# A two-stream transformer stack on one core: shift products with the shift as the stationary operand, and a re-ordered matrix-memory layer

## The reference, cut to what matters

```
def rms_norm_2(x):
    x32 = x.astype(jnp.float32)
    y = x32 * lax.rsqrt(jnp.mean(x32 * x32, axis=-1, keepdims=True) + EPS)
def modulate(h, shift, scale):
    return h * (1.0 + scale[:, None, :]) + shift[:, None, :]
...
for layer in range(DEPTH_2):
    mod = cond @ ada_w[layer] + ada_b[layer]
    sh1, sc1, g1, sh2, sc2, g2 = jnp.split(mod, 6, axis=-1)
    h = modulate(rms_norm_2(x), sh1, sc1)
    y = mixer(h)                       # pool and attention (layer 0), matrix memory (layer 1)
    x = x + g1[:, None, :] * y
    h = modulate(rms_norm_2(x), sh2, sc2)
    x = x + g2[:, None, :] * swiglu(h, ...)
```

## Time and profile before

| what | value |
|---|---|
| median of 3 runs | 1999.43 us (1997.7 to 1999.89) |
| the profiled execution, its own time | 1998.28 us |
| its span, from first to last instruction | 1996.5 us |
| PE busy | 1927.8 us, 97% |
| DVE, ACT, POOL busy | 938.3, 742.5, 771.6 us |
| mean granted TensorE clock | 0.985 of full speed |

### The profile page before, as it was taken

The page is one execution under the profiler, slowest core; times in us unless marked ns, Lnnn a source line. Parts: engine busy times, 40 slices in busy tenths (PEclk is TensorE's granted clock), DMA queues, the critical chain, the costliest instruction groups (busy, mean ns, idle before and its releaser), DMA issues.

```text
span 1996.5 us, 24687 instructions
## 1 busy us (share of the span) xinstructions
PE 1927.8 (97%) x9394; PEld 1572.7 (79%) x9394; DVE 938.3 (47%) x1227; ACT 742.5 (37%) x921; POOL 771.6 (39%) x225
## 2 busy tenths in 40 slices
PE   6999999989999999979989999999999999999999
PEld 5878778778888888845878888888988787888887
DVE  6244533676614544766776326637844272111111
ACT  5344424443322335236432222244357442222221
POOL 2322314434344444200334443444385344444433
PEclk9999999999999999989989999999999999999999
DMA  4211111436435524100445355422221222223222
GB/s 175 82 64 64 64 64 63 179 100 227 148 117 189 206 100 154 69 4 31 160 168 174 103 176 192 163 97 77 103 86 46 103 84 87 90 87 126 85 79 100
DMA packets 46365, 223.90 MB, mean 112 GB/s; under 512 B 4928, under 2 KB 9280, under 8 KB 31696
## 3 DMA queue, kind: packets, MB, share of 16 engines
q1 hardware_dynamic: 45856, 221.00, 32.4%
q10 hardware_dynamic: 432, 1.84, 0.3%
HBM read 220.68 MB, written 2.13 MB: 112 GB/s over the span
## 4 chain that ended last, share of the span: by engine, by line
PE 52%; issue 34%; POOL 7%; DVE 4%; ACT 2%; DMA 0%; POOLq 0%; DVEq 0%; SPq 0%; ACTq 0%
PE pairs L497 27%; PE pairs L521 10%; POOL wl L2118 7%; PE pairs L540 2%; PE pairs L512 2%; PE pairs L1913 2%; PE pairs L816 2%; DVE arena L438 2%; PE pairs L823 1%; PE pairs L479 1%; PE aux L1900 1%; ACT wh L458 0%; PE aux L881 0%; PE aux L869 0%; DVE xl L448 0%
## 5 line engine op out<-in xcount | busy, mean ns | idle before, releaser
L2118 POOL TENSOR_TENSOR wl<-raw,wh 128x2048 fp32r<-128x2048 f32 (+2 forms) x171 | 706.5, 4132 | 1187.9 <-ACT wh L458 1187.9
L497 PE MATMUL pairs<-xh,wh 128*128 128x512 f32 x1176 | 461.5, 392 | 8.7 <-POOL wl L2118 4.6
L497 PE MATMUL pairs<-xh,wl 128*128 128x512 f32 x1176 | 459.0, 390 | 0.0
L497 PE MATMUL pairs<-xl,wh 128*128 128x512 f32 x1176 | 458.8, 390 | 0.0
L458 ACT ACTIVATE wh<-raw 128x2048 fp32r<-128x2048 f32 x171 | 326.8, 1911 | 341.2 <-PE pairs L521 211.0
L497 PEld LDWEIGHTS pairs<-xh,wh 128*128 128x128 f32 x1176 | 221.7, 189 | 57.8 <-issue 5.3
L497 PEld LDWEIGHTS pairs<-xh,wl 128*128 128x128 f32 x1176 | 221.7, 189 | 46.8 <-issue 1.0
L497 PEld LDWEIGHTS pairs<-xl,wh 128*128 128x128 f32 x1176 | 221.6, 188 | 46.3
L521 PE MATMUL pairs<-zl,wh 128*128 128x512 f32 x518 | 201.6, 389 | 0.0
L521 PE MATMUL pairs<-zh,wl 128*128 128x512 f32 x518 | 201.5, 389 | 0.0
L521 PE MATMUL pairs<-zh,wh 128*128 128x512 f32 x518 | 201.5, 389 | 0.0
(11 more groups left out here) (316 smaller groups left out, 3015.3 us busy)
## 6 DMA issues: line engine op xcount, KB each, us to landing
raw<-in_w SPq DMA_DIRECT2D x113, 1024.0 KB, 5.0
arena<-in_ada SPq DMA_DIRECT2D x96, 512.0 KB, 4.4
raw<-in_w SPq DMA_DIRECT2D x48, 704.0 KB, 4.0
raw<-in_w SPq DMA_DIRECT2D x14, 512.0 KB, 3.7
arena<-mx_rows SPq DMA_DIRECT2D x16, 256.0 KB, 3.5
h<-in_xT SPq DMA_DIRECT2D x4, 512.0 KB, 8.6
outT<-h SPq DMA_DIRECT2D x8, 256.0 KB, 5.4
arena<-in_pool ACTq DMA_DIRECT2D x1, 1024.0 KB, 7.7
```

The costliest lines, as they stand in the source:

```text
L497: mm = p.matmul(pairs[:, 2 * slot + m, :], w[:, slot, at:at + P], src[part][:, k, :], start=(k == 0 and w is wh and part == 0), stop=(k == ...
L2118: g.tensor_tensor(wl[:, slot, 0:w], raw[:, slot, 0:w], wh[:, slot, 0:w].bitcast(F), ALU.subtract).then_inc(lo_done, 1)
```

## The change

It has five parts.

1. Shift products: the two shift columns are loaded as the stationary operand and the weights move, 256 columns at a time. This makes 8 x (wh, wl) = 16 products of 128x256 with a result on 2 partitions (high and low part in a row each). ACT copies that row pair from PSUM to the new tile `shr`, and two products with ones (K=2) turn it into one column per output tile, high and low added; DVE copies the two columns to `wsh`.
2. The place: the 16 products stand right behind `norm_sum_pe` (after k=2) and no longer after k=5; the two new small products stand after k=5. ACT's copy stands ahead of its loop over the tiles (L325).
3. Matrix-memory layer, first unit: its scores are made in the middle of the last `ml_v` chunk, POOL builds its exponents ahead of the low part of `ml_o` chunk 0, and DVE weights its scores ahead of draining that last chunk.
4. Bank pairs swapped: even units use the pair 1, odd units the pair 0. `values(0)` and `values(1)` wait for one chunk of `ml_v` each, and `ml_o` chunk 0 waits for the head sums of unit 14 only; those of unit 15 are waited for ahead of chunk 1.
5. The head copies (every fourth unit) stand behind the head sums and denominators of their round. (Three semaphores of `n_final` become one, with the same order of work.)

```diff
             c0 = C0[NORM_TO[name]]
+            if name in SHIFTED:
+                a.wait_ge(sh_mm, 2 * SHIFTED[name] + 1)
+                a.activation(shr[:, :], aux[0:2, 1, 0:256], ACT.Copy).then_inc(sh_row, 1)
             for k in range(KT):
...
         def shift_pe(p, name, slot):
             p.wait_ge(sh_lo, SHIFTED[name] + 1)
+            for k in range(KT):
+                for w in (wh, wl):
+                    mm = p.matmul(aux[0:2, 1, 0:256], shs[:, k, :], w[:, slot, k * 256:(k + 1) * 256],
+                                  start=(k == 0 and w is wh), stop=(k == KT - 1 and w is wl),
+                                  skip_group_check=True)
+            mm.then_inc(sh_mm, 1)
+
+        def shift_sum_pe(p, name):
+            p.wait_ge(sh_row, SHIFTED[name] + 1)
             for m in range(2):
-                for k in range(KT):
-                    at = k * 256 + m * P
-                    for w in (wh, wl):
-                        mm = p.matmul(aux[:, 1, 2 * m:2 * m + 2], w[:, slot, at:at + P], shs[:, k, :],
-                                      start=(k == 0 and w is wh), stop=(k == KT - 1 and w is wl),
-                                      skip_group_check=True)
+                mm = p.matmul(aux[:, 1, 256 + m:257 + m], shr[:, m * P:(m + 1) * P], cm("ones")[0:2, 0:1],
+                              start=True, stop=True, skip_group_check=True)
             mm.then_inc(sh_mm, 1)
...
                 if k == 2:
                     norm_sum_pe(p, name)
+                    if name in SHIFTED:
+                        shift_pe(p, name, slot)
                 if k == 5 and name in SHIFTED:
-                    shift_pe(p, name, slot)
+                    shift_sum_pe(p, name)
...
         def pv_bank(n):
-            return pairs[:, 2 * (n % 2):2 * (n % 2) + 2, :]
+            return pairs[:, 2 * ((n + 1) % 2):2 * ((n + 1) % 2) + 2, :]
...
             p.wait_ge(m_one, 1)
             for n in range(MN):
                 if n + 1 < MN:
-                    score(n + 1)
+                    ml_score_pe(p, n + 1)
+                if n < 2:
+                    p.wait_ge(drained, C_V + 3 + n)
                 values(n)
...
                 if stage == "ml_o":
-                    chunk_loop(g, stage, body, hi=1)
-                    ml_gpsimd(g)
+                    ml_gpsimd(g, mid=lambda: chunk_loop(g, stage, body, hi=1))
                     chunk_loop(g, stage, body, lo=1)
...
             turned_dve(v, 1)
+            ml_weighted_dve(v, 0)
             v_drain(v, 3)
...
-            linear_pe(p, "ml_v", lo=3)
+            linear_pe(p, "ml_v", lo=3, mid=lambda: ml_score_pe(p, 0))
             ml_pe(p)
-            p.wait_ge(k_hs, 2 * MN)
+            p.wait_ge(k_hs, 2 * (MN - 1))
             linear_pe(p, "ml_o", hi=1)
             for n in range(MN - 3, MN):
                 ml_turn_pe(p, n)
+            p.wait_ge(k_hs, 2 * MN)
             linear_pe(p, "ml_o", lo=1)
```

More of the change, by code:

```diff
@@ L310, in norm_act @@
                 a.activation(RSTD, LNV, ACT.Exp, scale=-0.5).then_inc(f_r1, 1)
-                a.wait_ge(f_ms, 1)
-                a.activation(LN2, LN2, ACT.Ln, scale=1.0 / D, bias=pc("eps")).then_inc(f_ln, 1)
-                a.wait_ge(f_sum, 1)
+                a.wait_ge(f_step, 2)
+                a.activation(LN2, LN2, ACT.Ln, scale=1.0 / D, bias=pc("eps")).then_inc(f_step, 1)
+                a.wait_ge(f_step, 4)
                 a.activation(RBOTH, LN2, ACT.Exp, scale=-0.5).then_inc(rstd_done, 1)
@@ L428, in norm_dve @@
                 v.wait_ge(f_r1, 1)
[L429 to L432, removed]
+                v.wait_ge(f_step, 1)
+                v.tensor_tensor(LN2, aux[:, 2, :], RBOTH, ALU.mult).then_inc(f_step, 1)
+                v.wait_ge(f_step, 3)
+                v.tensor_tensor(LN2, LN2, LNV, ALU.add).then_inc(f_step, 1)
             v.wait_ge(rstd_done, n + 1)
@@ L504, in body @@
                     for tb in range(TB):
+                        if tb == 2 and mid:
+                            mid()
                         if kind == "T":
@@ L1890, in ml_gpsimd, with ml_score_pe @@
                                 ).then_inc(k_a, 1)
-        def ml_pe(p):
-            def score(n):
-                pr, tb = n // TB, n % TB
-                if n:
-                    p.wait_ge(k_s, 2 * n)
-                for i in range(TB):
-                    for j in range(2):
-                        r = 64 * j
-                        mm = p.matmul(MS_PS[:, j, i, :], MQK[r:r + 64, 4 + pr, i * P:(i + 1) * P],
-                                      MQK[r:r + 64, pr, tb * P:(tb + 1) * P], start=True, stop=True,
-                                      skip_group_check=True)
-                mm.then_inc(scored, 1)
+                if n == 0:
+                    mid()
+        def ml_score_pe(p, n):
+            pr, tb = n // TB, n % TB
+            if n:
+                p.wait_ge(k_s, 2 * n)
+            else:
+                p.wait_ge(m_utc, 2)
+                p.wait_ge(m_silu, 4)
+            for i in range(TB):
+                for j in range(2):
+                    r = 64 * j
+                    mm = p.matmul(MS_PS[:, j, i, :], MQK[r:r + 64, 4 + pr, i * P:(i + 1) * P],
+                                  MQK[r:r + 64, pr, tb * P:(tb + 1) * P], start=True, stop=True,
+                                  skip_group_check=True)
+            mm.then_inc(scored, 1)
+        def ml_pe(p):
             def values(n):
@@ L1916, in values @@
                 mm.then_inc(valued, 1)
-            p.wait_ge(m_utc, 2)
-            p.wait_ge(m_silu, 4)
-            score(0)
-            p.wait_ge(drained, end_of("ml_v"))
             p.wait_ge(m_one, 1)
@@ L1970, in ml_act, with ml_weighted_dve @@
                     mm.then_inc(k_hn, 1)
+        def ml_weighted_dve(v, n):
+            tb = n % TB
+            v.wait_ge(k_e, n + 1)
+            v.wait_ge(scored, AN + n + 1)
+            for d, i0, i1 in ((0, 0, tb + 1), (1, tb, TB)):
+                e = ME[n % 3][:, :, d + i0:d + i1, :].rearrange("p j b t -> p j (b t)")
+                v.scalar_tensor_tensor(e, aux[:, 0:2, i0 * P:i1 * P], SB_D ** -0.5, e, ALU.mult, ALU.mult
+                                       ).then_inc(k_s, 1)
         def ml_dve(v):
@@ L2008, in ml_dve @@
                     v.reciprocal(M_RC[q % 3], M_DEN[q % 2]).then_inc(k_rc, 1)
+                if n % TB == TB - 1 and TB < n < MN:
+                    head_out(n // TB - 1)
             head_out(ML_H // 2 - 1)
```

26 lines of the change are left out of this document (9 added, 17 removed).

## The result

The changed kernel took 2005.17 us (median of 7 runs, 2001.46 to 2006.60), the kernel before 1997.70 us (median of 7 runs, 1991.76 to 1999.89). The ratio is 1.0049, 95% interval [1.0034, 1.0065]: slower by 7.5 us by the medians and by about 10 by the ratio. The median lies 0.3 us from the predicted one. The profiled execution took 2006.08 us (span 2004.3), against 1998.28 (span 1996.5) before: 7.8 us more.

A forecast was written before the change was run, and what follows sets the result against it. The prediction took PE, busy 97% of the span, as the bound. Norms +9.5, clock 0 and matrix-memory layer -3.3 made +6.2 us, for a forecast median of 2005.5 us, range 1998 to 2011.

The forecast's parts named there:

- Shift work: PE at each norm: 16 products in 1.9 us plus 0.3 for two sums replace 3.57, saving 1.4 us.
- The new place: Four norms: PE idles for the shift's low part ahead of tiles 3 to 5; 1.5 + 2.75 + 2.75 + 2.5 = +9.5 us.
- case D: Rival at the norms: two lowered clock stretches each and a late first-chunk chain; at most +6.8 us more, 2012; chance 0.07.
- Why L436 is long: Shift's low part at the norms: blocked on shared ports for POOL's whole subtraction, 4.56 to 4.61 us; otherwise short, no stall.
- Clock 0: Four norms: lower clock behind the stall costs the same as behind the two-column products; 0, bounds -6.8 to +6.8 us.
- Layer, -3.3: Matrix-memory layer: POOL's unit 15 done 1.0 later, but waits at the end go, chunk 1 earlier; -3.3 us, bounds -2 and -5.
- Sum: Whole kernel: +9.5 + 0 - 3.3 = +6.2 us, median 2005.5 us, 0.3% slower.
- B: Rival at the norms: no stall, each saves 1.4 of work and 1.7 of clock; 1983.7 us; chance 0.08.
- C: Rival at the norms: the stall comes but the clock stays up; -0.6 us, 1998.8; chance 0.14.

The follow-up runs named there:

- e9: Changed kernel with POOL's 128x2048 subtraction of the weights' low part cut into two halves; ratio 0.9977 to the kernel before.
- e1: Changed kernel with the 16 shift products put back behind tile 5 and the small sums behind tile 6; ratio 1.0001 to the kernel before.
- e2: Changed kernel with both shift parts made early by VectorE into buffers of their own; ratio 0.9968 to the kernel before.
- e5: Kernel before, old products in the old place, with only the shift parts made early by VectorE; ratio 1.0004 to the kernel before.
- e6: e2 with POOL making the low part of `ml_o` chunk 0 ahead of unit 0 again; ratio 0.9941 to the kernel before.
- e4: Kernel before with only the shift part of the change; ratio 1.0065 to the kernel before.
- e10: e6 with POOL's subtraction cut in halves as in e9; ratio 0.9944 to the kernel before.
- e7: e2 with the first chunk's renormalization and ACT's next high part moved later, to k=6; ratio 1.0014 to the kernel before.
- e8: e6 with the later steps of e7 added; ratio 0.9975 to the kernel before.
- e3: Kernel before with only the matrix-memory layer's part of the change; ratio 0.9999 to the kernel before.

## Why the prediction was right, point by point

- **Shift work, 1.4 us less per norm.** 16 products at the full clock took 1.82 us behind the waits of e9 and 1.87 in e1 (I took 1.9); the two small sums 0.53 instead of 0.3. 3.57 - 1.82 - 0.53 = 1.22. Right, with the sums under-sized by 0.2.
- **The new place, +9.5.** Mechanism right in each link: L436 not moved, blocked by POOL's instruction in four of four, PE idle 3.4 to 3.9 us ahead (predicted 3.6 to 4.1). Measured 1.81 + 2.82 + 4.31 + 2.70 = 11.6. Three norms agree with 1.5, 2.75 and 2.5 to 0.3 us; `n_o1` lost 4.31 where 2.75 stood. Of it 1.1 came through the lowered stretch of 6.8 us in place of 3.4 (from the low part's end to tile 6 it is 9.31 us there and 8.2 at the others), which the prediction held to be case D. And 2.4 came back behind `n_final` and `n_e2`, which no term had. Both misses nearly cancel, which is luck.
- **Why L436 is long.** Shown by e9 (half the instruction, half the wait) and e2 (0.17 us away from POOL). The rule of the Trainium skill's page "SBUF — State Buffer", part "SBUF: two separate sides", that the loser of the shared ports is blocked for the other's whole instruction, is the one that the trace agrees with: 4.47 us with one instruction of 4.50, 2.32 with one of 2.34. The runs show who is held and for how long; that a shared port is the reason, no run here shows by itself.
- **Clock 0.** Right in sum: in the four norms the clock was low for about 17 us before and after, but not norm by norm (before, `n_final` had two stretches; after, `n_o1` had the long one), so that the exact zero is luck too. The two causes are now separate: behind two-column products in e5, behind an idle 3.4 us or more in the changed kernel, behind neither in e9.
- **Layer, -3.3.** Measured -2.44. The end gained as predicted (a wait of 0.58 for 2.11, none for 1.54). The term under-sized is the loss at its beginning. Counted from the copies of the third value chunk, POOL began unit 3 2.25 us later than before (2.0 predicted) and ended unit 15 2.6 later (1.0 predicted): PE waited for POOL's unit behind the subtraction (4.64 us), did the score of unit 2 and the values of unit 1 at the lower clock (3.76 us instead of 2.50), and POOL then waited 1.29 us for PE at unit 4, which the sum had not.
- **Sum.** 11.6 - 2.4 - 2.44 + 1.0 (at marks where nothing was changed: 0.50 ahead of `n_final`, the rest between them) = 7.8 in the traces, +6.2 predicted; by the ratio it is about +10, so the loss was under-sized. That the median came out at 0.3 us from the forecast is luck: the kernel before measured 1997.70 in this comparison, 1.7 under the 1999.43 that the forecast started from.
- **Rivals.** B (no stall) and C (clock up) did not come. e2 is what B described, and it got 6.4 us of B's 15.7 (12.4 + 3.3): B left out the second chunk's tile 5, whose wait grew by some of what the first chunk gained, and kept the layer's term whole. The expectation of e1 left out the same tile. In the layer too there was more to gain than the forecast saw: it counted 2.0 us for POOL's subtraction between units 0 and 1, and without it (e6) the stretch to the low part of chunk 1 is 6.1 us shorter (81.74 against 87.83).

## What to carry to other kernels

Before a step is moved ahead on an in-order engine, look at the duration of what it waits for, however small: a subtraction of 8 columns at 4.5 us is a sign of something that it waits for inside, and filler work in front of the wait was hiding it. Take such small inputs out of the busy place altogether, then move. And when a wait is removed, read the next wait of the same engine first: here two chains ended within 2 us of each other. The new products in the old place (e1), and the early parts with the old products (e5), were worth nothing, the new products in the new place with late parts were a loss (e4), and all together were worth 0.3% (e2). Cutting the long instruction in two (e9, 0.9977) got most of that with the parts left late; it helps where one short instruction is held, and not where the next one in the chain is caught by the second half (e10).

## What the runs showed of the hardware

- A VectorE subtraction of 128x8 from two SBUF inputs lasted as long as the GpSimd subtraction that it started 0.04 us behind: 4.47 of 4.50, 2.32 of 2.34; 0.17 us alone. In the three norms of e9 where it was held, GpSimd's next instruction, queued right behind, didn't shut it out again.
- A VectorE tile instruction of 0.75 us with two SBUF inputs that started inside a GpSimd subtraction ended 0.55 us behind that one's end, at all four norms of all twelve traces, however late it had started. VectorE's steps on PSUM were not: the copy of two columns to `wsh` took 0.15 us inside GpSimd's subtraction (e2, at 1367.70 within 1367.18 to 1371.77) and 0.15 ahead of one (e7, at 1383.27 ahead of 1384.20).
- The hold goes both ways: GpSimd's subtraction took 4.86 and 5.00 us in place of 4.50 and 4.62 where its recorded start lay inside a VectorE instruction with two SBUF inputs (`n_e2` of the changed kernel and of the one before).
- TensorE's waits of 3.2 to 4.4 us at the norms (the changed kernel, e1, e4, e7, e8) came with 3.4 or 6.8 us at a granted clock of 0.5, the 1.2 GHz level, in 19 of 20 places; a wait of 3.40 us at `n_o1` in e8 did not. The seven waits of 1.0 to 1.8 us at the norms in e9 (1.03, 1.66 and 1.44 ahead of the products; 1.57, 1.75, 1.09 and 1.09 at tile 5) came with none. Between them it went either way: in e2 a wait of 2.88 us was not followed by the lower clock, one of 1.91 was, and so was the one of 1.80 in the kernel before. Cutting the waits was thus worth more than the idle time that went: 14 us for 10.5.
- 32 products that move two columns brought the lower clock too, with TensorE never idle, in 11 of 12 places (the kernel before, e3, e5; not at `n_o1` in e3). Behind 16 that move 256 columns (0.12 us each) and didn't wait, it never fell (the four norms of e1).
